# High and low parts of the tokens side by side: one matmul of 512 columns in place of two of 256

## The reference

```
y[t] = sum over the experts e that token t picked:  gate[t, e] * gelu(x1[t] . u[e]) * v[e]
x    = LayerNorm(alpha * x1 + y)
```

## Time and profile before

| | |
|---|---|
| median of 3 runs | 1536.66 us (1536.66 to 1539.16) |
| profiled execution | 1539.63 us, span 1537.8 us |
| mean granted TensorE clock | 0.945 of full speed |
| TensorE / DVE / ScalarE / GpSimd busy | 1403.0 / 871.2 / 527.7 / 288.1 us |
| one-hot stage | about 721 to 836 us |
| first half of the loop | 843.41 to about 1160 us |
| second half, and the last LayerNorm | 1162.75 to 1537.8 us |

### The profile page before, as it was taken

The page is one execution under the profiler, slowest core; times in us unless marked ns, Lnnn a source line. Parts: engine busy times, 40 slices in busy tenths (PEclk is TensorE's granted clock), DMA queues, the critical chain, the costliest instruction groups (busy, mean ns, idle before and its releaser), DMA issues.

```text
span 1537.8 us, 26735 instructions
## 1 busy us (share of the span) xinstructions
PE 1403.0 (91%) x8955; PEld 1150.1 (75%) x8956; DVE 871.2 (57%) x2128; ACT 527.7 (34%) x1002; POOL 288.1 (19%) x557
## 2 busy tenths in 40 slices
PE   7979997878888989994999999999999999999974
PEld 6869897554456456783998888999987888888853
DVE  3440001765443319975996788888885555555436
ACT  3411001543332111111333454544454444444422
POOL 0112222200000116651000111111111122211222
PEclk9989998788888989997999999999999999999987
DMA  7877887403887314353792999999996888888861
GB/s 241 296 243 251 303 285 263 172 1 127 304 318 270 144 53 155 101 164 147 187 245 80 309 315 314 314 313 319 314 314 212 286 289 294 281 275 286 296 210 64
DMA packets 158045, 359.55 MB, mean 234 GB/s; under 512 B 50579, under 2 KB 92435, under 8 KB 154259
## 3 DMA queue, kind: packets, MB, share of 16 engines
q1 hardware_dynamic: 125970, 239.37, 46.5%
q0 software_dynamic: 25088, 112.93, 21.0%
q10 hardware_dynamic: 6912, 6.29, 1.2%
HBM read 342.08 MB, written 53.61 MB: 257 GB/s over the span
## 4 chain that ended last, share of the span: by engine, by line
PE 50%; DVE 1%; DMA 1%; POOL 1%; issue 0%; ACT 0%; DVEq 0%; ACTq 0%; SPq 0%; POOLq 0%
PE psum L1544 23%; PE psum L1534 6%; PE psum L1533 6%; PE psum L1532 6%; PE psum L1079 4%; PE psum L1557 3%; PE psum L1569 2%; DMA early_u<-in_peer_u 1%; DMA gathered<-in_peer_v,v_rows_of 0%; POOL gathered L1775 0%; DVE ln_bn L1034 0%; DVE x L1068 0%; DVE x L1029 0%; POOL gathered L1780 0%; DVE x L1066 0%
## 5 line engine op out<-in xcount | busy, mean ns | idle before, releaser
L1707 DVE TENSOR_TENSOR v_lo<-big,v_hi 128x1024 fp32r<-128x1024 f32 x128 | 156.8, 1225 | 115.5 <-ACT v_hi L1624 91.6
L1533 PE MATMUL psum<-x_lo,u_hi 128*128 128x256 f32 x760 | 215.0, 283 | 0.0
L1534 PE MATMUL psum<-x_hi,u_lo 128*128 128x256 f32 x760 | 215.0, 283 | 0.0
L1532 PE MATMUL psum<-x_hi,u_hi 128*128 128x256 f32 x760 | 214.8, 283 | 0.0
L1624 ACT ACTIVATE v_hi<-big 128x1024 fp32r<-128x1024 f32 x128 | 135.3, 1057 | 140.2 <-PE psum L1544 108.9
L1544 PE MATMUL psum<-v_hi,gated_hi 128*128 128x512 f32 x512 | 162.6, 399 | 6.7 <-DVE gated_lo L1732 6.7
L1544 PE MATMUL psum<-v_lo,gated_hi 128*128 128x512 f32 x512 | 160.1, 394 | 0.0
L1544 PE MATMUL psum<-v_hi,gated_lo 128*128 128x512 f32 x512 | 159.4, 393 | 0.0
L1533 PEld LDWEIGHTS psum<-x_lo,u_hi 128*128 128x128 f32 x760 | 145.5, 191 | 3.7
L1532 PEld LDWEIGHTS psum<-x_hi,u_hi 128*128 128x128 f32 x760 | 145.5, 191 | 3.7
L1534 PEld LDWEIGHTS psum<-x_hi,u_lo 128*128 128x128 f32 x760 | 145.5, 191 | 0.0
(11 more groups left out here) (308 smaller groups left out, 2401.6 us busy)
## 6 DMA issues: line engine op xcount, KB each, us to landing
big<-in_peer_v SPq DMA_DIRECT2D x128, 512.0 KB
big<-in_peer_u SPq DMA_DIRECT2D x112, 512.0 KB, 3.9
big<-in_a_k SPq DMA_DIRECT2D x8, 2048.0 KB, 11.9
a_vals<-in_a_v SPq DMA_DIRECT2D x8, 2048.0 KB
keep_ak<-in_a_k POOLq DMA_DIRECT2D x32, 508.0 KB, 6.2
keep_av<-in_a_v POOLq DMA_DIRECT2D x24, 512.0 KB, 6.7
sel_pages<-in_sel_pool SPq DMA_DIRECT2D x64, 128.0 KB, 2.8
wq_ring<-in_peer_wq SPq DMA_DIRECT2D x16, 512.0 KB, 3.7
```

What stands on the lines that cost most here:

```text
L1532: pe.matmul(H[:, 0:SEQ], uh[:, q, kc], x1h[:, k, :], start=(k == 0), stop=False)
L1533: pe.matmul(H[:, 0:SEQ], uh[:, q, kc], x1l[:, k, :], start=False, stop=False)
L1534: mm = pe.matmul(H[:, 0:SEQ], ul[:, q, kc], x1h[:, k, :], start=False, stop=(k == KD - 1))
L1707: ve.tensor_tensor(vl[:, q], vs[:, q], vh[:, q].bitcast(F32), ALU.subtract).then_inc(s["v_lo"], 1)
```

## The change

x1h and x1l become the two halves of one tile, x1_parts: for each k the 256 high columns and behind them the 256 low ones. In P1, one matmul of 512 columns multiplies uh with both into the whole bank H; ul with x1h still is a matmul of 256 into columns 0 to 255. Its place in the order is one k ahead. The low half, columns 256 to 511, is then added by hand: ScalarE copies columns 0 to 255 to SBUF, DVE adds columns 256 to 511 from PSUM, ScalarE takes the Gelu in place. P1 waits for DVE's add where it waited for the Gelu. On DVE the add stands last in the body of a position with k % 4. For unit 0, ScalarE's part moves from group 1 to group 2 of the one-hot stage, and DVE's add is put after group 2.

```diff
-                act.activation(hg[:, q], H[:, 0:SEQ], ACT.Gelu_apprx_tanh).then_inc(s["gelu"], 1)
+                act.activation(hg[:, q], H[:, 0:SEQ], ACT.Copy).then_inc(s["h_half"], 1)
+                act.wait_ge(s["h_sum"], n + 1)
+                act.activation(hg[:, q], hg[:, q], ACT.Gelu_apprx_tanh).then_inc(s["gelu"], 1)
...
                 pe.wait_ge(s["u_lo"], n + 1)
-                pe.wait_ge(s["gelu"], n)
+                if not isinstance(n, int) or n:
+                    pe.wait_ge(s["h_sum"], n)
                 for k in range(KD):
                     kc = slice(k * P, (k + 1) * P)
-                    pe.matmul(H[:, 0:SEQ], uh[:, q, kc], x1h[:, k, :], start=(k == 0), stop=False)
-                    pe.matmul(H[:, 0:SEQ], uh[:, q, kc], x1l[:, k, :], start=False, stop=False)
-                    mm = pe.matmul(H[:, 0:SEQ], ul[:, q, kc], x1h[:, k, :], start=False, stop=(k == KD - 1))
+                    mm = pe.matmul(H, uh[:, q, kc], t.x1p[:, k].rearrange("p e n -> p (e n)"), start=(k == 0), stop=(k == KD - 1), skip_group_check=True)
+                    if k < KD - 1:
+                        pe.matmul(H[:, 0:SEQ], ul[:, q, k * P + P:k * P + 2 * P], x1h[:, k + 1, :], start=False, stop=False, skip_group_check=True)
+                    if k == 0:
+                        pe.matmul(H[:, 0:SEQ], ul[:, q, kc], x1h[:, k, :], start=False, stop=False, skip_group_check=True)
...
+            def h_sum(n, m):
+
+                ve.wait_ge(s["h_half"], n + 1)
+                ve.tensor_tensor(hg[:, m], hg[:, m], H[:, SEQ:2 * SEQ], ALU.add).then_inc(s["h_sum"], 1)
...
                 if g == 1:
                     u_lo(0, 0)
                     u_lo(1, 1)
+                if g == 2:
+                    h_sum(0, 0)
...
                     ve.tensor_tensor_reduce(junk[:], gr[:, k % 4], t.x1[:, 2, :], 1.0, 0.0, ALU.mult, ALU.add, h4[:, k % 4:k % 4 + 1]).then_inc(s["dots"], 1)
+                if k % 4 and left > 1:
+                    h_sum(n + 1, 1 - m)
...
-                if g == 1:
+                if g == 2:
                     hidden(0, 0)
```

More of the change, by code:

```diff
@@ L1251, in _ @@
                 if g == 0:
-                    act.activation(t.x1h[:], xT[:, :, 0:SEQ], ACT.Copy).then_inc(s["x_hi"], 1)
+                    act.activation(t.x1h, xT[:, :, 0:SEQ], ACT.Copy).then_inc(s["x_hi"], 1)
             for n in range(len(after_unit), EARLY_R):
@@ L1294, in _ @@
                     gp.wait_ge(s["x_hi"], 1)
-                    gp.tensor_tensor(t.x1l[:], xT[:, :, 0:SEQ], t.x1h[:].bitcast(F32), ALU.subtract).then_inc(s["x_lo"], 1)
+                    gp.tensor_tensor(t.x1l, xT[:, :, 0:SEQ], t.x1h.bitcast(F32), ALU.subtract).then_inc(s["x_lo"], 1)
         @block.vector
@@ L1580, in _ @@
                 if g == 1:
[L1581 to L1587, removed]
+                    product1(0, 0)
             product1(1, 1)
@@ L1903 @@
 W_out onehot zero iota_in st_y""".split()
-LATE_SEMS = """x1_twice ld_g0 ld_g1 ld_g2 ld_g3 dots dots_kept n_gelu n_gate n_turn n_turned v_mm v_clear v_gates st_w0 st_w1 ld_w0 ld_w1
+LATE_SEMS = """x1_twice ld_g0 ld_g1 ld_g2 ld_g3 dots dots_kept n_gelu h_sum h_half n_gate n_turn n_turned v_mm v_clear v_gates st_w0 st_w1 ld_w0 ld_w1
 ld_p0 ld_p1 ld_p2 ld_p3 ld_e0 ld_e1 hp_mm hp_out st_h0 st_h1 ld_h0 ld_h1 gelu_p""".split()
@@ L1943, in build @@
         t.hp = sb("early_hidden", [P, 2, SEQ])
-        t.x1h, t.x1l = sb("x1_hi", [P, KD, SEQ], F32R), sb("x1_lo", [P, KD, SEQ], F32R)
+        t.x1p = sb("x1_parts", [P, KD, 2, SEQ], F32R)
+        t.x1h, t.x1l = t.x1p[:, :, 0], t.x1p[:, :, 1]
         t.i1 = sb("i1", [P, SEQ])
```

## The result

The changed kernel takes 1561.24 us (median of 4 runs, 1558.09 to 1564.17), the kernel before 1536.66 us. The ratio is 1.0155, 95% interval 1.0129 to 1.0181: 20 to 28 us slower. The forecast was 1560. The four runs of the changed kernel lie 6 us apart, so that the median came within 1.2 us of the forecast is partly luck; what tests the forecast is the division by stages. The profiled execution of the changed kernel has a span of 1556.2 us, 18.4 us more than before.

What follows compares the result with a forecast made beforehand. TensorE bound both halves before; after the change, DVE-ScalarE hand-overs would set the first half. 7.3 (before the loop) + 19.7 (first half) - 4.5 (second half) + 0.9 (tail) = +23.4 us, giving 1560 us, range 1541 to 1575.

Steps and rivals of the forecast that it cites:

- The bound before: Expert loop before the change: bound by TensorE in both halves, groups of 19.58 us and 21.62 us.
- The hand-overs: First half: DVE to ScalarE to DVE cycle takes 20.96 us a group against 19.29 of TensorE work; +19.7 us.
- Rival 1: First half: TensorE stays the bound, DVE's spare time holds the adds, 19.29 us a group; 1536 us in all; chance 0.07.
- Rival 3: First half: hand-overs at about half the price, period 20.1 us, +9.6 in all, 1546 us; chance 0.11.
- rival 2: Loop bound by TensorE and unit 0's copy early, so step 24 does not stall: 1529 us, faster; chance 0.06.
- The stall at step 24: One-hot stage: DVE waits for unit 0's add, step 24 starts 5.2 us late at half clock; +7.3 us.
- The step on P1 of unit 1 lying beside the store and load: Loop opening: this P1 runs beside the opening store and load, so its saving is left out.
- The extra 1.0 us of the first group: First half: low clock at the loop's start still delays the first group's P1; plus 1.0 us.
- the k=3 term: First half, k=3: ScalarE copies the four dots first, so the add starts 0.77 us after DVE is ready; 6.37 us.
- TensorE's saving: P1: one 512 and one 256 matmul replace three of 256, 0.097 us a P1; second half -4.5 us.
- The tail: After the last P1: copy, add and two hand-overs more on the chain through the last gated_lo; +0.9 us.
- Rival 4: First half: clock falls in TensorE's idle pieces, mean 0.85, 22.7 us a group, +27 more, 1588 us; chance 0.07.

Runs made afterwards that it cites:

- e2: Changed kernel without ScalarE's copy and DVE's add, Gelu straight from PSUM at its old place, wide matmul kept: 1530.05 us, ratio 0.9954 to the kernel before.
- e5: Changed kernel with three matmuls of 256 columns a k again in P1; copy, add and Gelu kept: 1563.65 us, ratio 1.0173 to the kernel before.
- e9: Changed kernel with one more add of the same shape, result unused, before each of DVE's adds: 1577.91 us, ratio 1.0278 to the kernel before.
- e7: Changed kernel with ScalarE's copy of the four dot products behind the copy of H and both Gelus: 1552.38 us, ratio 1.0092 to the kernel before.
- e3: Changed kernel with the dots' copy moved as in e7 and DVE's add ahead of the dot product: 1542.09 us, ratio 1.0025 to the kernel before.
- e8: Changed kernel with e3's add order, the dots' copy on GpSimd, unit 0's add and Gelu after group 3: 1530.66 us, ratio 0.9964 to the kernel before.
- e1: Changed kernel with unit 0's copy, add and Gelu after group 3 of the one-hot stage: 1556.12 us, ratio 1.0116 to the kernel before.

## Why the prediction was right

- *The bound before.* TensorE in both halves, as e2 shows: less TensorE work alone makes both periods shorter, by 0.20 and 0.19 us.
- *The hand-overs.* Right in mechanism and size: 5.60, 6.31 and 9.00 us for 5.60, 6.37 and 8.99. That they are a cycle of its own is shown by e5 (TensorE's work given back: the same period) and e9 (three adds more, 0.99 us between starts: 0.99 us a group more). That the order makes them one is shown by e7, e3 and e8. Rival 1 (DVE has spare time, so the adds fit) is refuted for the order given, and holds for e8's. Rival 3 (hand-overs at half the price) is refuted by the same four adds, and rival 2 by the first half and by step 24 both.
- *The stall at step 24.* 5.2 us late and a low clock after it, 7.7 us for the 7.3 forecast. The pair took 6.11 us where the forecast had 5.8. e1 removes it. (By its own terms the early product behind it would end at 822.2, not 822.3, and the stall without a fall of the clock would be 6.5 us, not 6.7; neither slip is in the sum.) The step on P1 of unit 1 lying beside the store and load was right for the changed kernel, but e1 shows how little cover that is.
- *The extra 1.0 us of the first group* did not come. Its gated_lo starts 20.92 us before the second group's (846.17 and 867.09), like all others: P1 was late within it and nobody waited. With the group 0.04 us too long (20.96 for 20.92, most of it the k=3 term), 16 times, this is the 1.6 us by which the first half was over-forecast.
- *TensorE's saving* was mis-sized: 0.067 us a P1, not 0.097. In the first half it doesn't matter, since it is hidden; in the second it gives 0.19 us a group for 0.28, so with 46 P1 3.1 us in place of 4.5. That the second half came out at -3.0 us for -3.6 all the same is luck: 1.6 us of it is the clock at the turn, which was no term of the sum. The tail and about 0.8 us more went the other way. The 0.8 us lie around the stop for the sample rows' gathers (from 1467.2 us before, 1484.2 after), where two groups together became 0.5 us longer; why is open.
- *The tail.* From the P2 pair of the last four positions to the last P2 the chain takes 12.41 us (1520.49 to 1532.90) where it took 11.55 before, +0.9 as forecast.
- *Rival 4* (the clock falls in the pieces) is refuted by the granted clock of 1.00 from 848 to 1180 us.

## What to carry to other kernels

A new step that crosses engines can cost far more by its place in their streams than by its length. Write out, for one period, the cycle of waits through the engines that hand over to each other, and compare it with the bound's work; an engine that is busy 82% of the time can lie on the cycle that sets the pace. Put the hand-over ahead of long independent work (here the dot product), and put no copy that waits for a late result in front of the step that others wait for. The same arithmetic was 1.6% slower or 0.4% faster than before, by the place of its steps alone: their order, and in the faster kernel one copy of four columns on another engine.

## What the runs showed of the hardware

In a P1 of the new form, a matmul of 512 columns and one of 256 with other weights together take 0.351 us, against 0.360 for three of 256 and 0.348 as the sum of one in P2 (0.228) and one in the old P1 (0.120): merging two matmuls of 256 columns saved 0.009 us. A ScalarE instruction of 4 columns lets the next start 0.11 us after it (1051.56 to 1051.67). An add with one operand in PSUM took 0.42 us for 128x256, as long as the subtraction gated_lo of the same shape from SBUF. Standing for 5.2 us cost TensorE more than these 5.2 us: the pair of steps behind it ran at a granted clock of 0.50 at first and took 6.11 us for 3.57.
